# Deferred modulation panels: row sums on VectorE inside turned 32 x 32 squares, the four quadrants on TensorE

## The reference, cut to what matters

```
def modulation(cond, w_mod, b_mod):
    m = jax.nn.silu(cond) @ w_mod + b_mod
    m = m.reshape(-1, 1, 3 * D_MODEL)
    return jnp.split(m, 3, axis=-1)
...
    shift, scale, gate = modulation(c, w_mod[layer], b_mod[layer])
    shift_c, scale_c, gate_c = modulation(c_ctx, w_mod[layer], b_mod[layer])
    h = rms_norm(x, norm_w[layer]) * (1.0 + scale) + shift
    hc = rms_norm(xc, norm_w[layer]) * (1.0 + scale_c) + shift_c
```

## Time and profile before

| what | value |
|---|---|
| median of three runs | 3478.27 us (3469.82 to 3486.32) |
| the profiled execution, first to last instruction | 3481.7 us |
| TensorE busy | 3318.7 us, 95% |
| VectorE busy | 2240.0 us, 64% |
| ScalarE busy | 1839.3 us, 53% |
| stretch in which the deferred panels are made | about 147 to 720 us |
| matmul records of L832 | 224 (112 matmuls) |

### The profile page before, as it was taken

How to read it: one execution, slowest core, us unless ns; L and a number is a source line. 1 busy time by engine, 2 the same in 40 slices (tenths; PEclk the granted TensorE clock), 3 DMA queues, 4 the chain that set the end, 5 groups by cost and what they waited for, 6 DMA issues and landing times.

```text
span 3481.7 us, 55238 instructions
## 1 busy us (share of the span) xinstructions
PE 3318.7 (95%) x22787; PEld 2952.9 (85%) x22787; DVE 2240.0 (64%) x3060; ACT 1839.3 (53%) x2892; POOL 475.0 (14%) x739
## 2 busy tenths in 40 slices
PE   7999999999899999999999998999998999899997
PEld 3588888888688999999999887888888998799996
DVE  3587777642545456676666667666666555799866
ACT  2344434232456745777676345555536564678644
POOL 0010011101000000000000012777220000222002
PEclk9999999999999999999999999999999999999999
DMA  9754456642233555555554554666554434455454
GB/s 359 250 182 163 171 194 216 230 139 97 76 126 133 169 178 194 181 181 176 187 181 154 174 182 167 208 206 202 180 181 141 140 130 161 156 170 168 159 180 148
DMA packets 174889, 608.45 MB, mean 175 GB/s; under 512 B 21840, under 2 KB 21872, under 8 KB 172848
## 3 DMA queue, kind: packets, MB, share of 16 engines
q1 hardware_dynamic: 145440, 495.54, 42.0%
q0 software_dynamic: 28624, 107.29, 9.0%
q10 hardware_dynamic: 576, 2.10, 0.2%
HBM read 596.27 MB, written 8.57 MB: 174 GB/s over the span
## 4 chain that ended last, share of the span: by engine, by line
PE 76%; DVE 8%; ACT 7%; DMA 6%; issue 3%; SPq 0%; ACTq 0%; DVEq 0%
PE psum_all L573 21%; PE psum_all L569 16%; PE psum_all L571 16%; PE psum_all L566 11%; DMA raw<-in_stream 5%; ACT w_hi L496 2%; DVE w_lo L503 2%; DMA mod_early<-in_stream 1%; PE psum_all L832 1%; PE psum_all L1480 1%; ACT ssd_seg L2208 1%; DVE xT L855 1%; PE psum_all L1450 1%; PE psum_all L731 1%; DVE ln_d L1056 1%
## 5 line engine op out<-in xcount | busy, mean ns | idle before, releaser
L573 PE MATMUL psum_all<-act_parts,w_lo 128*128 128x256 f32 (+1 forms) x6704 | 2014.1, 300 | 0.0
L503 DVE TENSOR_TENSOR w_lo<-raw,w_hi 128x1024 fp32r<-128x1024 f32 x866 | 1067.1, 1246 | 880.1 <-ACT w_hi L496 879.2
L569 PE MATMUL psum_all<-act_parts,w_hi 128*128 128x256 f32 (+1 forms) x4464 | 1413.0, 317 | 43.6 <-DVE act_parts L952 33.9
L571 PE MATMUL psum_all<-act_parts,w_hi 128*128 128x256 f32 (+1 forms) x4464 | 1383.4, 310 | 0.0
L496 ACT ACTIVATE w_hi<-raw 128x1024 fp32r<-128x1024 f32 x866 | 907.9, 1056 | 809.1 <-DMA raw<-in_stream 806.9
L573 PEld LDWEIGHTS psum_all<-act_parts,w_lo 128*128 128x128 f32 x6704 | 1287.4, 192 | 43.0
L569 PEld LDWEIGHTS psum_all<-act_parts,w_hi 128*128 128x128 f32 x4464 | 861.2, 193 | 115.4 <-issue 51.6
L571 PEld LDWEIGHTS psum_all<-act_parts,w_hi 128*128 128x128 f32 x4464 | 861.8, 193 | 43.9 <-issue 3.4
L566 PE MATMUL psum_all<-act_parts,w_hi 128*128 128x512 f32 x2240 | 803.3, 402 | 29.1 <-DVE w_lo L503 15.6
L566 PEld LDWEIGHTS psum_all<-act_parts,w_hi 128*128 128x128 f32 x2240 | 424.7, 190 | 137.5 <-issue 24.8
L855 DVE SCALAR_TENSOR_TENSOR xT<-mod_late,small,xT 128x1024 f32<-128x1024 f32 x210 | 256.5, 1279 | 2.9 <-DMA mod_late<-in_stream 0.6
(11 more groups left out here) (488 smaller groups left out, 3422.8 us busy)
## 6 DMA issues: line engine op xcount, KB each, us to landing
raw<-in_stream SPq DMA_DIRECT2D x858, 512.0 KB, 3.3
mod_late<-in_stream POOLq DMA_DIRECT2D x128, 512.0 KB, 4.4
mod_early<-in_stream SPq DMA_DIRECT2D x128, 256.0 KB, 6.5
ssd_seg<-acs_rows POOLq DMA_DIRECT2D x8, 1536.0 KB, 7.0
s_matrices<-s5p_made POOLq DMA_DIRECT2D x16, 384.0 KB, 3.9
raw<-in_stream SPq DMA_DIRECT2D x16, 256.0 KB, 4.7
s_made<-s_matrices POOLq DMA_DIRECT2D x16, 256.0 KB, 3.0
xT<-in_x SPq DMA_DIRECT2D x1, 2048.0 KB, 10.2
```

Of the source, the lines that this page charges most:

```text
L503: dve.tensor_tensor(w_lo[:, n % RING, :], raw[:, n % RING, :], w_hi[:, n % RING, :].bitcast(F32), ALU.subtract).then_inc(lo_ready, 1)
L569: pe.matmul(sums, w_hi[:, n % RING, cols], block.rhs(kk, HIGH, block.width), start=(kk == 0), stop=False)
L571: pe.matmul(sums, w_hi[:, n % RING, cols], block.rhs(kk, LOW, block.width), start=False, stop=False)
L573: last = pe.matmul(sums, w_lo[:, n % RING, cols], block.rhs(kk, HIGH, block.width), start=False, stop=(kk == block.kt - 1))
```

## The change

VectorE gets a new step `late_reduce` behind the last unit of a panel. It waits for the sums, turns every 32 x 32 square of each 128 x 1024 sum in place of its row (`transpose`, into the other panel's sums, which are free then), and adds up each square's rows along the free axis (`reduce_sum`, 128 x 1024 to 128 x 32). It waits for its own transposes before the reductions, and for the reductions at its end. What is left for TensorE is to add the four groups of 32 partitions: `quadrants` is a 128 x 32 matrix with a one wherever the partition is m modulo 32, made once at the start, and four matmuls with 16 (or 8) moving columns write the four quadrants of a bank. `late_mod_add` is `mod_add` for the new layout of the bank. The wait for TensorE in `late_add` goes; one for the panel two before stands in `late_reduce` in its place.

```
@@ prepare_vector
+            dve.reduce_sum(quadrants, const("ident").rearrange("p (a m) -> p m a", m=32), AX_X)
...
         def late_tensor(pe, slot):
             p = late_turned(slot)
             if p is not None:
-                pe.wait_ge(late_summed, late_sums_before((p + 1) * KT))
+                n = late_conditions(p)
+                pe.wait_ge(late_reduced.sem, late_reduced.at(p + 1))
                 if p >= 2:
                     pe.wait_ge(mod_added, 4 + p - 1)
-                for v in range(late_conditions(p)):
-                    for h in range(2):
-                        for b in range(4):
-                            at = 4 * b + 2 * h + v
-                            last = pe.matmul(psum[6 + p % 2][:, at:at + 1],
-                                             late_sums[p % 2][v][:, (4 * h + b) * P:(4 * h + b + 1) * P],
-                                             const("ones", 0, 1), start=True, stop=True)
+                for c in range(4):
+                    last = pe.matmul(psum[6 + p % 2][32 * c:32 * c + 32, 0:8 * n], quadrants,
+                                     late_rows[:, p % 2, 0:n, :].rearrange("p v (k c) -> p v k c", c=4)[:, :, :, c],
+                                     start=True, stop=True)
                 last.then_inc(mod_turned, 1)
+
+        def late_reduce(dve, p):
+            ordered, n = order["vector"], late_conditions(p)
+            dve.wait_ge(late_summed, late_sums_before((p + 1) * KT))
+            for v in range(n):
+                turned = late_sums[1 - p % 2][v]
+                dve.transpose(turned, late_sums[p % 2][v]).then_inc(ordered.sem, 1)
+                at = ordered.step()
+            dve.wait_ge(ordered.sem, at)
+            if p >= 2:
+                dve.wait_ge(mod_turned, 4 + p - 1)
+            for v in range(n):
+                last = dve.reduce_sum(late_rows[:, p % 2, v, :],
+                                      late_sums[1 - p % 2][v].rearrange("p (b i) -> p b i", i=32), AX_X)
+            last.then_inc(late_reduced.sem, 1)
+            dve.wait_ge(late_reduced.sem, late_reduced.at(p + 1))
...
         def late_add(dve, i):
...
-                if k == 0 and p >= 2:
-                    dve.wait_ge(mod_turned, 4 + p - 1)
...
         def late_vector(dve, slot):
             i = pair_after(slot)
             if i is not None:
                 late_add(dve, i)
+                if i % PAIRS == PAIRS - 1:
+                    late_reduce(dve, i // PAIRS)
             p = late_turned(slot)
             if p is not None:
                 layer, in_layer = LATE_PAIRS[p * PAIRS][0:2]
-                mod_add(dve, layer, in_layer, 4 + p, 6 + p % 2, late_conditions(p))
+                late_mod_add(dve, layer, in_layer, p)
```

More of the change, by code:

```diff
@@ L673, in build @@
         fold = small[:, 0:4].rearrange("p (h v) -> p h v", v=2)
+        quadrants = small[:, 128:160]
+        late_rows = at_work("mod_late_rows", [P, 2, 2, 32], 80)
         early_units = [ring[:, i, :] for ring in (at_act("mod_early_0", [P, 4, UNIT], 16), at_act("mod_early_1", [P, 4, UNIT], 48),
@@ L749, in mod_turn @@
             last.then_inc(mod_turned, 1)
[L751 to L757, removed]
         modulated = signal("early_modulated", 4)
@@ L820, in late_turned @@
             return panel_ended(slot - LATE_LAG)
+        late_reduced = signal("late_reduced", len(LATE_PAIRS) // PAIRS)
         def late_tensor(pe, slot):
@@ new lines, in late_mod_add @@
+        def late_mod_add(dve, layer, in_layer, p):
+            n = late_conditions(p)
+            dve.wait_ge(mod_turned, 4 + p + 1)
+            a = layer * 96 + in_layer * 16
+            out, bias = (x.rearrange("p (k v) -> p v k", v=2)[:, 0:n, :]
+                         for x in (modulation[:, a:a + 16], param("b_mod", a, a + 16)))
+            sums = psum[6 + p % 2][:, 0:8 * n].rearrange("p (v k) -> p v k", v=n)
+            dve.tensor_tensor(out, sums, bias, ALU.add).then_inc(mod_added, 1)
```

## The result

The changed kernel takes 3448.93 us (median, 3438.61 to 3453.01), the kernel before 3478.27 (3469.53 to 3486.32) beside it: a ratio of 0.992, 95% interval 0.990 to 0.9941. These are the lines of the page of the changed kernel that answer to the table and to the earlier trace rows: the span, busy time of TensorE and VectorE, the chain.

A forecast was written before the change was run, and what follows sets the result against it. TensorE was taken to set the pace, with VectorE following. Terms: -23.2 - 7.7 + 0 + 15.8 = -15.1 us, profiled execution 3481.7 to 3466.6, median 3463 us; range 3451 to 3476.

The forecast's parts named there:

- What TensorE loses: At all eight panels' ends, TensorE's batches shrink from 30.9 to 7.7 us, a gain of 23.2 us (21.0 to 26.4).
- I take 7.7, since the step is not set by the width alone: TensorE's 64 remaining records keep the old step of 0.12 us each, 7.7 us in all (ends 4.5 and 9.9).
- The clock among the gating blocks: Three half-clock stretches behind the batches at 474, 538 and 603 us go: 7.7 us gained (0 to 7.7).
- The clock among the attention blocks: Some half-clock stretches go, others come behind the new waits: balance 0, 5 us either way.
- The block: VectorE's two transposes and two reductions per two-condition panel, 1.2 us each plus 0.2 of waits: 5.0 us (4.1 to 16.6).
- B: VectorE's transposes run at half the ordinary pace, 2.3 us each; sum -6.0, 3472 us; chance 0.17.
- C: VectorE becomes the bound at panels 0, 1, 2 and 4, transposes 4.7 us each; sum +18, 3496 us; chance 0.06.
- Its waits: TensorE waits for VectorE at panels 0, 1, 2 and 4: 4.8 + 5.0 + 3.15 + 1.0 + 1.8 = 15.8 us.
- Slack nothing: 5.0 us: At panel 1 TensorE already waits for VectorE's probabilities, so VectorE's whole 5.0 us of new work becomes wait.
- the second wait: After panel 2 VectorE stays late, so TensorE waits 1.0 us more for the next probabilities.
- Rival A: Faster transposes (waits 12.2 us) and 5 us of clock gained among the attention blocks; sum -23.7, 3455 us; chance 0.24.
- Rival D: TensorE's gain is lost to waiting for the next unit's DMA and ScalarE; 3478 less a few; chance 0.05.

The follow-up runs named there:

- first pair of profiles: The first profiled executions of the kernel before (span 3481.7 us) and of the changed kernel, whose runs measured 3448.93 us, ratio 0.992.
- sixteen narrow matmuls: Changed kernel with 16 idle matmuls, 32-column weights in one quadrant, ahead of each of the first six batches: 3461.84 us, 0.9959 of the kernel before.
- sixteen wide ones: Changed kernel with 16 idle matmuls, 128-column weights, ahead of each of the first six batches: 3490.4 us, 1.0058 of the kernel before.
- panel 0 alone: Kernel before with VectorE's transposes and reductions added at panel 0 only, one execution: 3485.63 us.
- second profile of before: Nothing changed: the kernel before profiled again, run 3472.6 us, span 3470.5 us.
- second pair: Both kernels profiled again, unchanged: the kernel before with a span of 3470.5 us, the changed kernel at 3448.34 us, ratio 0.9928.

## Why the prediction was wrong

The direction, the places and, over all runs, the clock were right; the time came out below the range because the sizes of two terms were off, both to the same side, and because of 3 us and more in later layers. By the steps of the prediction, against the first pair of profiles:

- **What TensorE loses (23.2 forecast): 25.5.** From a batch's first weight load to the next line's, before took 31.4 us for all eight and the changed kernel 3.4, of which 1.9 are idle time behind the last one; the longer idle time ahead of each of the eight (0.35 for 0.04) takes 2.5 of the gain. The step that failed is "I take 7.7, since the step is not set by the width alone". The records take 2.07 us, far under the ends that I gave (0.07 to 0.15 a record); with the 0.35 us ahead of each batch, which I had not thought of, it is 4.3 us without the last one's wait. The sixteen narrow matmuls against sixteen wide ones show that width does set most of the step. I had bounded it by the duration of a single load (111 ns), although loads overlap; the duration of the new ones is the same (0.11 us), but eight of them start within 0.05 us.
  The Trainium skill has it: "TensorE: Matmul & The Clock Gate", section "LDWEIGHTS (loading the stationary operand)", gives a load's time in ns as its columns divided by 1.2, which as an estimate from that page is 107 ns for 128 columns and 27 for 32; the measured steps of 0.11 and 0.031 us agree. Its "Part 3: Packing small matmuls" says that matmuls at different tile positions run at the same time; the 0.26 us for eight records fit that. I had not weighed these two.
- **The clock among the gating blocks (7.7): 7.8.** All three stretches went, in every profile with the short batch alone. 20.5 us at half clock are 10.2 lost, of which 2.4 lay inside the batches (4.86, 4.06 and 4.52 against 3.68 us). Sixteen wide matmuls brought two short ones back.
- **The clock among the attention blocks (0, 5 either way): 3.3 gained** (5.1 less 1.8 inside the batches) in the first pair, none in the second. Nothing but the execution separates these: before itself had 37.5 and 17.1 us. Over all runs the whole change gives 9 us of clock, about what the gating stretches lost, so the term was right to stand at 0, and its bound right too. It is the balance of two larger ones: taking the block out gives 9 us of clock, so the short batches must have saved about as much there as the block's waits cost.
- **The block (5.0 us): 4.8.** Right, and rivals B and C fall with it.
- **Its waits (15.8): 10.3**, the largest miss. Panel 0: 4.8, as forecast. Panel 1: forecast "Slack nothing: 5.0 us", measured 3.77 where there had been 2.31, so 1.5 more. The step that failed is taking an idle time of one execution for a fixed property of the place: the 2.31 us came from a unit that arrived late, and without it VectorE is 1.1 us early there (4.8 less 3.7), as panel 0 alone and the second profile of before confirm. Against a profile without that accident the block costs 3.7. Panel 2: 3.0 for 3.15, and the second wait, forecast at 1.0, did not come (the 0.35 us there are those ahead of every batch). Panel 4: 1.0 for 1.8, though other executions with this block have 0.3 to 2.2 there. Panels 3, 5, 6 and 7: nothing, as forecast.
- **Sum.** -25.5 - 7.8 - 3.3 + 10.3 = -26.3, against 27.9 measured in layer 0 and 30.8 between the spans. The rest, 3 us here and 6 in the second pair, lies in later layers, where both programs do the same. That part varied between 2752 and 2769 us over all profiles, and I can't say whether the change has a share in it. By their sizes the misses are 5.5 us of waits, 2.3 of the batches, 3.3 of clock that the first pair of executions gave by chance, 1.6 that the pieces don't account for, and those 3 us, whose cause stays open.

Rival A came nearer with its sum (-23.7), for the wrong reason: transposes at the fast pace. In its other half, more clock, it was right for the first pair only. Rival D falls: apart from the 1.0 us at panel 4, TensorE waited for no unit in place of a batch. The rule of the Trainium skill that I weighed ("TensorE: Matmul & The Clock Gate", on gaps that get the engine throttled) agrees with the runs in the main: with the block the waits at panels 0 and 2 had a stretch at 0.50 behind them in both profiles, and without the block the attention blocks had 6.8 us instead of 17.1 to 27.3. Taken strictly it goes too far: in the second profile the 3.7 us wait at panel 1 had none.

## What to carry to other kernels

Where TensorE adds up with matmuls of few moving columns, the width of their weights is most of the price: shrink the weights, put the pieces in quadrants of their own, and reckon with some 0.3 us more of idle time ahead of each batch. Work handed from the bound engine to a follower costs what is left of it after the slack at each place, so read the slack there, and read it in more than one execution: an idle time that a late DMA made is no property of the place. And compare two kernels at full clock and in clock lost separately, since the second part alone moved 12 us between two executions of one kernel.

## What the hardware did that I had not expected

- Loads and matmuls of 32-column weights: 0.031 us a record in one quadrant, and eight records over four quadrants in 0.26 us; with 128 columns 0.11. Ahead of each of the eight batches the weight loads stood idle for 0.35 us. A load's own duration in the trace (0.11 and 0.19 us) does not show this.
- Turning the 32 x 32 squares of 128 x 1024 float32 values took 1227 ns, the pace of L503 (1221 ns), so here it cost nothing extra.
- The same program spent 58 us of layer 0's two stretches at half clock in one execution and 34 in another, with spans of 3481.7 and 3470.5 us.
